# Sixteen tokens set apart in an expert layer: from one token's experts on the partitions to head and token on the partitions

## What is computed

```python
def block(xb):
    q = (xb @ w_query).reshape(TB, PH, 2, PEER_QUERY_DIM // 2)
    s = jnp.einsum('thpd,hpkd->thpk', q, sub_keys).astype(jnp.float32)
    v_half, i_half = lax.top_k(s, K)
    ...
    idx = jnp.take_along_axis(cidx.reshape(TB, PH, K * K), pos, axis=-1)
    g = jax.nn.softmax(top_s, axis=-1).astype(xb.dtype)
    u = expert_u[idx]
    a = jax.nn.gelu(jnp.einsum('td,thkd->thk', xb, u), approximate=False)
    return jnp.einsum('thk,thkd->td', g * a, expert_v[idx])
```

## Time and profile before

| | us |
|---|---|
| median of 3 runs (963.35 to 964.4) | 963.48 |
| the profiled execution, its own time | 963.28 |
| its span, first to last instruction | 961.4 |
| TensorE busy in the span | 953.2 |
| VectorE busy | 762.9 |
| ScalarE busy | 556.3 |
| GpSimd busy | 339.2 |

### The profile page before, as it was taken

The page is one execution under the profiler, slowest core; times in us unless marked ns, Lnnn a source line. Parts: engine busy times, 40 slices in busy tenths (PEclk is TensorE's granted clock), DMA queues, the critical chain, the costliest instruction groups (busy, mean ns, idle before and its releaser), DMA issues.

```text
span 961.4 us, 22318 instructions
## 1 busy us (share of the span) xinstructions
PE 953.2 (99%) x7649; PEld 916.4 (95%) x7649; DVE 762.9 (79%) x1606; ACT 556.3 (58%) x995; POOL 339.2 (35%) x202
## 2 busy tenths in 40 slices
PE   9999999999999999999999999999999999999997
PEld 9999899999999999999999999999899899898997
DVE  7988868879799997877778765878778777677776
ACT  6556764666665647676666764555455455454545
POOL 0000000076877788888888882010001000000000
PEclk9999999999999999999999999999999999999999
DMA  8877568766678899999999998999999999899981
GB/s 302 266 234 205 192 210 239 235 183 200 185 228 245 251 228 310 305 251 297 297 265 296 292 271 260 345 328 335 297 316 318 353 292 314 270 309 297 267 260 45
DMA packets 134080, 254.56 MB, mean 265 GB/s; under 512 B 29856, under 2 KB 78880, under 8 KB 133744
## 3 DMA queue, kind: packets, MB, share of 16 engines
q1 hardware_dynamic: 112192, 235.57, 76.7%
q0 software_dynamic: 21376, 17.12, 9.2%
q10 hardware_dynamic: 432, 0.80, 0.3%
HBM read 227.07 MB, written 26.35 MB: 264 GB/s over the span
## 4 chain that ended last, share of the span: by engine, by line
PE 94%; DVE 3%; DMA 1%; ACT 1%; issue 1%; DVEq 0%; ACTq 0%
PE pOO L1462 44%; PE pSS L1762 9%; PE pOO L1741 8%; PE pTT L1758 6%; PE pMM L1758 6%; PE pOO L1758 6%; PE pOO L1759 3%; PE pMM L1759 3%; PE pTT L1759 3%; DVE wlos L937 1%; PE pSS L1527 1%; PE pSS L1788 1%; PE pSS L1683 1%; PE pTT L1716 1%; PE pSS L1716 1%
## 5 line engine op out<-in xcount | busy, mean ns | idle before, releaser
L669 ACT ACTIVATE whis<-raw 128x1024 fp32r<-128x1024 f32 x326 | 344.0, 1057 | 201.0 <-PE pSS L1762 164.3
L1462 PE MATMUL pOO<-xhi,whis 128*128 128x240 f32 (+1 forms) x1040 | 288.2, 277 | 0.0
L1462 PE MATMUL pOO<-xhi,wlos 128*128 128x240 f32 (+1 forms) x1040 | 286.1, 275 | 0.0
L1462 PE MATMUL pOO<-xlo,whis 128*128 128x240 f32 (+1 forms) x1040 | 286.0, 275 | 0.0
L937 DVE TENSOR_TENSOR wlos<-raw,whis 128x1024 fp32r<-128x1024 f32 x172 | 208.8, 1219 | 38.8 <-ACT whis L669 38.2
L1353 DVE TENSOR_TENSOR wlos<-raw,whis 128x1024 fp32r<-128x1024 f32 x125 | 153.2, 1225 | 80.8 <-ACT whis L669 80.8
L644 POOL DMA_INDIRECT g_scratch<-small x112 | 201.9, 1802 | 41.4 <-issue 32.3
L1462 PEld LDWEIGHTS pOO<-xhi,whis 128*128 128x128 f32 x1040 | 196.3, 189 | 1.5 <-issue 1.3
L1462 PEld LDWEIGHTS pOO<-xhi,wlos 128*128 128x128 f32 x1040 | 196.4, 189 | 0.0
L1462 PEld LDWEIGHTS pOO<-xlo,whis 128*128 128x128 f32 x1040 | 196.3, 189 | 0.0
L605 POOL TENSOR_TENSOR wlos<-raw,whis 128x1024 fp32r<-128x1024 f32 x30 | 72.1, 2412 | 214.4 <-ACT whis L669 214.3
(11 more groups left out here) (297 smaller groups left out, 2007.2 us busy)
## 6 DMA issues: line engine op xcount, KB each, us to landing
raw<-in_stream SPq DMA_DIRECT2D x199, 512.0 KB, 4.8
raw<-in_vrows SPq DMA_DIRECT2D x128, 512.0 KB, 5.0
a_scratch<-ast SPq DMA_DIRECT2D x128, 120.0 KB, 3.5
held<-a_scratch SPq DMA_DIRECT2D x128, 120.0 KB, 4.7
g_scratch<-ghot SPq DMA_DIRECT2D x32, 256.0 KB, 4.6
held<-x_scratch SPq DMA_DIRECT2D x16, 512.0 KB, 6.0
held<-g_scratch SPq DMA_DIRECT2D x124, 64.0 KB, 4.5
biasm<-in_bias SPq DMA_DIRECT2D x8, 256.0 KB, 5.6
```

Source lines behind the costliest of these rows:

```text
L669: act.activation(whi[s], raw[s][:], ACT.Copy).then_inc(hi_ready, 1)
L1462: last = pe.matmul(dst, st, mv, start=(c == 0 and q == 0), stop=(c == len(terms) - 1 and q == 2))
```

## The change

The 16 tokens are laid out by head and token: partition h x 16 + t holds head h of token t, and the gather j takes pick j of all 128 pairs of head and token, 16 gathers as before. So one copy of the 16 rows of x, laid eight times (`xall`), serves all dot products. It is loaded once, with eight DMAs of 16 rows each, in `load_apart` after U tile 46's load and tile 41's store on SP; eight DMAs before those bring the picks and gates of the tokens from `route` into that layout (`picks`). VectorE makes the offsets from them at tile 46 (`offsets_apart`). The dots are 14 in the U stage and 2 in the V stage; GpSimd's gathers of U rows come three at a time before the heads 3 to 6 and two before the head 7.

In the V stage VectorE adds each gathered block of V rows, times its share per partition, into `yacc` (`add_row`, 128 x 1024), one after each group in ROW_GROUPS. The four rounds on TensorE, their shares spread over a zeroed tile, and ScalarE's copy are gone; the eight pairs of matmuls at tile 120 sum over the heads with `chosen`. The bank that this frees lets the chunks 6 and 7 be done like the others, with 480 and 240 columns. In the tail, the parts of the chunks 6 and 7 are added in two steps each, chunk 7's before the last block of tiles has ended, and the transposes go to other banks. The diff, cut to its core:

```diff
-GROUPS = 4
-PER_GROUP = APART // GROUPS
-DOTS_U = 12
-RANKS_U = DOTS_U // GROUPS
-DOT_TILES_U = (49, 55, 65, 68, 79, 84, 92, 97, 105, 111, 119, 124)
-XROW_AT = 6
+DOTS_U = 14
+DOT_TILES_U = (57, 60, 65, 73, 76, 81, 89, 92, 97, 105, 108, 113, 121, 124)
+GATHERS_U = {3: (0, 1, 2), 4: (3, 4, 5), 5: (6, 7, 8), 6: (9, 10, 11), 7: (12, 13)}
+APART_AT = 46
+OFFSETS_AT = 46
-DOT_TILES = (10, 22, 38, 50)
-DOT_GROUPS = (4, 7, 11, 14)
-GELU_GROUPS = (2, 16)
-SHARE_GROUPS = (3, 17)
+DOT_TILES = (10, 20)
+DOT_GROUPS = (4, 7)
+GELU_GROUPS = (2, 9)
+SHARE_GROUPS = (3, 11)
 ROW_TILES = (2, 9, 16, 23, 33, 39, 45, 51, 57, 63, 69, 75, 81, 87, 93, 99)
-ROUND_TILES = (32, 56, 80, 104)
+ROW_GROUPS = (5, 6, 8, 9, 10, 12, 13, 15, 16, 18, 19, 21, 22, 24, 25, 27)
-WIDE = 6
-SLOT = P // GROUPS
...
-        xrow = [piece(80 + 8 * s, 8) for s in range(4)]
-        ysum = xrow[0][:, 0:512]
-        shares = piece(112, 5)[:, 0:SLOT // 2 + APART * SLOT]
-        shares_at = shares[:, SLOT // 2:].rearrange("p (j n) -> p j n", j=GROUPS)[:, :, 0:(PER_GROUP - 1) * (SLOT + 1) + 1:SLOT + 1]
+        xall = piece(80, 8)
+        yacc = piece(88, 8)
...
-        uoff = small[:, 2, 0:APART].bitcast(U32)
-        share1 = small[:, 2, APART:2 * APART]
-        dots = small[:, 2, 2 * APART:3 * APART]
-        chosen = [small[:, 3, q * APART:(q + 1) * APART] for q in range(2)]
+        uoff = small[:, 2, 0:TOPK].bitcast(U32)
+        dots = small[:, 2, TOPK:2 * TOPK]
+        shares = small[:, 2, 2 * TOPK:3 * TOPK]
+        picks = small[:, 2, 3 * TOPK:6 * TOPK].rearrange("p (a k) -> p a k", a=3)
+        chosen = small[:, 3, 0:APART]
...
-        wide_pairs = [pTT, pMM, pOO]
-        wide = [wide_pairs[c // 2][:, c % 2, 0:2 * NU].rearrange("p (q n) -> p q n", q=2) for c in range(WIDE)]
-        acc = [wide_pairs[c // 2][:, c % 2, NU:NU + T] for c in range(WIDE)] + [pS[1][:, q * T:(q + 1) * T] for q in range(2)]
+        wide_pairs = [pTT, pMM, pOO, pSS]
+        wide = [wide_pairs[c // 2][:, c % 2, 0:2 * NU].rearrange("p (q n) -> p q n", q=2) for c in range(C)]
+        acc = [wide_pairs[c // 2][:, c % 2, NU:NU + T] for c in range(C)]
         end7 = pM[1][:, 0:NU]
-        ends = [[pSS[:, q, :] for q in range(2)], [pTT[:, q, :] for q in range(2)]]
+        ends = [[pT[0], pO[1]], [pT[1], pS[1]]]
...
-            def load_xrow(j):
-
-                if j >= 4:
-                    sp.wait_ge(dots_done, j - 3)
-                sp.dma_start(xrow[j % 4], x_dram[row_token(j):row_token(j) + 1, :].to_broadcast([P, D])).then_inc(xrow_landed[j % 4], 16)
+            def load_apart():
+
+                sp.wait_ge(routed, 1)
+                for h in range(PH):
+                    sp.dma_start(picks[h * APART:(h + 1) * APART], route[P - APART:P, 1, :, h, :]).then_inc(picks_landed, 16)
+                sp.wait_ge(xtok_stored, 16)
+                sp.wait_ge(gbanks_free, 2)
+                for h in range(PH):
+                    sp.dma_start(xall[h * APART:(h + 1) * APART], x_dram).then_inc(x_landed_apart, 16)
...
-                j = dot_at(t - T_U + XROW_AT)
-                if j is not None:
-                    if j == 0:
-                        sp.wait_ge(xtok_stored, 16)
-                        sp.wait_ge(gbanks_free, 2)
-                    load_xrow(j)
+                if t == T_U + APART_AT:
+                    load_apart()
...
                 if j >= U_BUFS:
                     pool.wait_ge(dots_done, j - U_BUFS + 1)
-                s = row_token(j)
-                pool.indirect_dma_start(urow[j % U_BUFS], None, urows, bass.IndirectOffsetOnAxis(uoff[:, s:s + 1], 0)).then_inc(urow_landed[j % U_BUFS], 16)
+                pool.indirect_dma_start(urow[j % U_BUFS], None, urows, bass.IndirectOffsetOnAxis(uoff[:, j:j + 1], 0)).then_inc(urow_landed[j % U_BUFS], 16)
             def gather_v(m):
-                r = m // GROUPS
-                if r:
-                    pool.wait_ge(rounds_done, r)
-                s = row_token(m)
-                pool.indirect_dma_start(urow[U_BUFS + m % V_BUFS], None, picked, bass.IndirectOffsetOnAxis(uoff[:, s:s + 1], 0)).then_inc(urow_landed[U_BUFS + m % V_BUFS], 16)
+                if m >= V_BUFS:
+                    pool.wait_ge(rows_added, m - V_BUFS + 1)
+                pool.indirect_dma_start(urow[U_BUFS + m % V_BUFS], None, picked, bass.IndirectOffsetOnAxis(uoff[:, m:m + 1], 0)).then_inc(urow_landed[U_BUFS + m % V_BUFS], 16)
...
-                if h == 2:
+                if h in GATHERS_U:
                     pool.wait_ge(uoff_ready, 1)
                     pool.wait_ge(gbanks_free, 2)
-                if h >= 2:
-                    gather_u(2 * (h - 2))
-                    gather_u(2 * (h - 2) + 1)
+                    for j in GATHERS_U[h]:
+                        gather_u(j)
...
-            groups(GELU_GROUPS[1], TAKE_GROUP)
-            act.wait_ge(rounds_done, PER_GROUP)
-            act.activation(ysum, pS[0], ACT.Copy).then_inc(ysum_ready, 1)
-            groups(TAKE_GROUP, NE_TILES // 4 - 1)
+            groups(GELU_GROUPS[1], NE_TILES // 4 - 1)
...
-
-            dve.scalar_tensor_tensor(uoff, routeT[:, 0, P - APART:P], float(NK), routeT[:, 1, P - APART:P], ALU.mult, ALU.add).then_inc(uoff_ready, 1)
-            link(dve.tensor_copy(share1, routeT[:, 2, P - APART:P]))
...
+            def offsets_apart():
+
+                dve.wait_ge(picks_landed, 16 * PH)
+                dve.scalar_tensor_tensor(uoff, picks[:, 0, :], float(NK), picks[:, 1, :], ALU.mult, ALU.add).then_inc(uoff_ready, 1)
+
             def dot(j):
-                dve.wait_ge(xrow_landed[j % 4], 16 * (j // 4 + 1))
+                dve.wait_ge(x_landed_apart, 16 * PH)
                 dve.wait_ge(urow_landed[j % U_BUFS], 16 * (j // U_BUFS + 1))
-                dve.scalar_tensor_tensor(urow[j % U_BUFS], urow[j % U_BUFS], 1.0, xrow[j % 4], ALU.mult, ALU.mult, accum_out=dots[:, j:j + 1]).then_inc(dots_done, 1)
+                dve.scalar_tensor_tensor(urow[j % U_BUFS], urow[j % U_BUFS], 1.0, xall, ALU.mult, ALU.mult, accum_out=dots[:, j:j + 1]).then_inc(dots_done, 1)
             def gates_apart(part):
-                if part == 0:
-                    link(dve.memset(shares, 0.0))
                 dve.wait_ge(dots_gelu, part + 1)
-                ranks = slice(RANKS_U, PER_GROUP) if part else slice(0, RANKS_U)
-                dve.tensor_tensor(shares_at[:, :, ranks], share1.rearrange("p (j q) -> p j q", j=GROUPS)[:, :, ranks],
-                                  dots.rearrange("p (q j) -> p j q", j=GROUPS)[:, :, ranks], ALU.mult).then_inc(shares_ready, 1)
+                at = slice(DOTS_U, TOPK) if part else slice(0, DOTS_U)
+                dve.tensor_tensor(shares[:, at], picks[:, 2, at], dots[:, at], ALU.mult).then_inc(shares_ready, 1)
+
+            def add_row(m):
+
+                row = urow[U_BUFS + m % V_BUFS]
+                dve.wait_ge(shares_ready, 1 if m < DOTS_U else 2)
+                dve.wait_ge(urow_landed[U_BUFS + m % V_BUFS], 16 * (m // V_BUFS + 1))
+                if m == 0:
+                    dve.tensor_scalar(yacc, row, shares[:, 0:1], None, ALU.mult).then_inc(rows_added, 1)
+                else:
+                    dve.wait_ge(rows_added, m)
+                    dve.scalar_tensor_tensor(yacc, row, shares[:, m:m + 1], yacc, ALU.mult, ALU.add).then_inc(rows_added, 1)
...
                 j = dot_at(i)
+                if i == OFFSETS_AT:
+                    offsets_apart()
                 if j is not None:
                     dot(j)
...
-            groups(1, SHARE_GROUPS[0])
-            gates_apart(0)
-            first = SHARE_GROUPS[0]
-            for j, end in enumerate(DOT_GROUPS):
+            first = 1
+            for end in range(1, TAKE_GROUP):
+                busy = end in DOT_GROUPS or end in ROW_GROUPS or end + 1 in SHARE_GROUPS
+                if not busy:
+                    continue
                 groups(first, end + 1)
-                dot(DOTS_U + j)
                 first = end + 1
-            groups(first, SHARE_GROUPS[1])
-            gates_apart(1)
-            groups(SHARE_GROUPS[1], NE_TILES // 4 - 1)
+                if first in SHARE_GROUPS:
+                    gates_apart(SHARE_GROUPS.index(first))
+                if end in DOT_GROUPS:
+                    dot(DOTS_U + DOT_GROUPS.index(end))
+                if end in ROW_GROUPS:
+                    add_row(ROW_GROUPS.index(end))
+            groups(first, NE_TILES // 4 - 1)
...
+            dve.wait_ge(tile_done, T_V + NE_TILES - BY_BLOCK)
+            link(dve.tensor_tensor(hT[:, 7, :], acc[7], hT[:, 7, :], ALU.add))
+            link(dve.tensor_tensor(hT[:, 7, 0:NU], wide[7][:, 0, :], hT[:, 7, 0:NU], ALU.add))
...
-            dve.tensor_tensor(hT[:, 6:8, :], pS[1].rearrange("p (h t) -> p h t", h=2), hT[:, 6:8, :], ALU.add).then_inc(h2_ready, 1)
-            dve.wait_ge(h2_ready, 4)
+            link(dve.tensor_tensor(hT[:, 6, :], acc[6], hT[:, 6, :], ALU.add))
```

(35 more changed lines are left out.)

36 lines of the change are left out of this document (14 added, 22 removed).

## The result

The changed kernel takes 970.14 us (median of 8 runs, 966.60 to 972.60) against 964.35 (963.35 to 965.17) for the kernel before on the same chip: a ratio of 1.006, 95% interval 1.0042 to 1.0079. It is 0.6% slower, where I had forecast 956.2, so the prediction was wrong by 13.9 us and in its sign. The profiled execution took 972.24, its span is 970.4, and its mean granted clock 0.989.

What follows compares the result with a forecast made beforehand. The prediction took TensorE's queue to bound the kernel. Its terms, -8.2 - 1.9 - 0.2 + 3.0 = -7.3 us, gave 956.2 us against the median of 963.48, with a range of 953.2 to 959.6.

Steps and rivals of the forecast that it cites:

- The rounds: V stage: four rounds leave TensorE's chain, where nothing covers them, at 2.05 us each: 8.2 us less.
- The wide form: V stage: chunks 6 and 7 with 480 and 240 columns save one of three matmuls, 0.0075 us per chunk and tile: 1.9 us less.
- Additions, gates and GpSimd's gathers in the V stage: V stage: VectorE's sixteen additions, 1.22 us each, fit its slack, gates add about 0.2, gathers come early enough: cost 0.
- the tail: After the V tiles: the additions for chunks 6 and 7 are hidden under TensorE's work: 0, at most 0.3 us.
- Tile 49: U stage: the 0.2 us this tile lost behind a `whi` waiting for its load should go: 0.2 us less.
- The burst: U stage: 16 DMAs on SP, 0.465 us per issue, delay load 47, so tile 46 starts 3.0 us late (0.9 to 5.3).
- The rival that spoke of 6 to 9 us: U stage: late load 47 also delays `wlo` 47 and a step of G, small descriptors slow the engines: 959.2 to 962.2; chance 0.08.
- DMA becomes the limit: V stage: waits for loads give back a third to a half of the gain: 959.6 to 961.4 us; chance 0.08.
- a hidden burst: U stage, rival: issues are shorter than thought and load 47 is still in time, so no stall: 953.2 us; chance 0.15.

Runs made afterwards that it cites:

- the paced kernel with spread loads: The changed kernel with `load_apart`'s 16 loads spread over tiles 46 to 57 and at most three of head 0's scatters in flight: 950.61 to 951.71 us, 0.988 of the kernel before.

## Why the prediction was wrong

- *The rounds, -8.2.* Right. The V stage is 10.7 us shorter, and 2.5 of it belongs to the next term. A tile with a round took 4.59 us and the one behind it 0.10 more than usual, 2.05 us for the two over 2 x 2.647, as worked out.
- *The wide form, -1.9.* Right in kind, 0.6 too small: -2.5.
- *Additions, gates and GpSimd's gathers in the V stage, 0; the tail, 0.* Right. The tail behind the last chunk is 0.14 us shorter.
- *Tile 49, -0.2.* Right. Without the burst, in the paced kernel with spread loads, it is 246.8 us from tile 41 to the V stage, where the kernel before has 247.0.
- *The burst, +3.0 (bounds 0.9 to 5.3).* The mechanism was right, place and order of waits too; the size was not. The failed step is the price of an issue: I had taken 0.465 us from a burst of loads out of DRAM. The eight loads of `picks`, from one SBUF tile to another in runs of 64 bytes, took 6.36 us in the changed kernel, 0.59 each but for two, and the eight of `x` 3.96:

```profile
372.90 6.36 SPq L512 DMA_DIRECT2D small<-route  x8
379.39 3.96 SPq L516 DMA_DIRECT2D held<-x_scratch  x8
383.39 0.42 SPq L472 DMA_DIRECT2D raw<-in_stream  x1
```

  So 10.5 us instead of 7.4. The second failed step is that I priced the idle time alone. Behind it the clock is lower: tile 46 took 4.82 us for 2.68. Tile 46 starts 20.0 us after tile 41 instead of 14.35, 5.7 us of idle time, and with the 2.1 of the slower clock the burst costs 7.8 us in this trace, 4.8 over the forecast. The rival that spoke of 6 to 9 us had the size, at 0.08, but not the mechanism: no step of G was late. That it was near is luck.
- *The pause near 300 us, 12 to 14 us.* Not in the forecast or in any rival. The step that failed is the part that costed the edit of `chosen` at nothing, by leaving it out: two small copies for one reduction in an engine with slack. I had looked at what each added operation delays, and for a removed one at nothing but its own time. The 2.1 us that VectorE gained let loads and scatters go out earlier, and in the sets that pause TensorE then stalls inside a tile and its signals come late. The forecast's picture, in which TensorE loses time only where another engine makes it wait, has no place for such a stall; how it comes about stays open. The rival "DMA becomes the limit" looked at the V stage, and in the pause the DMA engines are idle.
- *Sum.* Without any burst and without the pause the kernel is at 950.8, where the forecast had 953.2 for a hidden burst: 12.0 us under the kernel before on the same chip (962.80), where the forecast had 10.3 under its own. By the traces of that chip the V stage gives 10.7 of the 12.0, with 0.6 from the wide form that the forecast lacks. The U stage gives 0.8, where it had 0.2. The start of the U stage is 0.4 earlier and the tail 0.1 shorter. The other 0.7 us of the distance from 953.2 is the chip: the kernel before took 963.48 when the forecast was made.

## What to carry to other kernels

An operation taken out of an engine with slack can still cost: follow what goes out earlier because of it, and what that meets. A group of DMA issues in one queue is priced by the form of its own transfers, and a stall of TensorE by its idle time and the slow clock behind it. Where a row of small scatters runs beside a TensorE that has no slack, try it with few of them in flight; here, with three, none of four runs paused, and it cost nothing. Where whole sets of runs are slower than others, compare how complete their traces are before you blame the kernel. And an idle DMA queue is no proof that it was shut out: look first whether anything was left in it.

## What the hardware showed that I had not expected

- During a row of 16 scatters TensorE can stall between matmuls of one tile that wait for nothing in the program (0.7 to 1.0 us, five times in one tile), and the signal of a finished tile can come 1.6 to 4.7 us late, where 0.01 is usual. It comes only in sets of runs whose traces have lost records of semaphores, and with it a kernel has two times 11 to 14 us apart.
- The same two copies of 128x16 took 2.45 us at 255 us, beside an unbroken row of GpSimd's operations of 2.4 us, and 0.25 us in the V stage, where GpSimd was idle; multiplications in their place took 2.46. VectorE's timeline of the kernel before with the copies moved:

```profile
647.30 0.25 DVE L1330 COPY small<-small 128x16 f32<-128x16 f32 x2
```

  The Trainium skill ("Trainium Architecture — The Big Picture", section What this means for kernel authors) says that the two engines share one pair of ports and that it is an exclusive lock. The trace agrees with it for these operations; the reduction at the same place took 0.37. (The moved copies read another tile, so place and source differ together.)
